# First mixer's attention: values held still, turned probabilities streamed, heads written turned, GpSimd divides

## The reference, cut to what matters

```
def window_attention(q, k, v, k_ctx, v_ctx, sink):      # 8 heads of 64, 2 key/value heads, blocks of 128 queries
    s_loc = einsum(q, k) * scale, -inf outside |qpos - kpos| <= 128
    s_ctx = einsum(q, k_ctx) * scale                    # 256 context keys
    p = softmax(concat[s_loc, s_ctx, sink])[..., :-1]
    return p_loc @ v + p_ctx @ v_ctx

def attn_gmlp_mixer(h, hc, w_in, w_out, ...):
    q, k, v, ua, va = split(h @ w_in);  q, k = axial_rope(q), axial_rope(k)
    kc, vc = split(hc @ w_in[:, Q_W:Q_W + 2 * KV_W])
    attn = window_attention(q, k, v, kc, vc, sink)
    mix = chunk_gmlp(ua, va, w_s, b_s)                  # gelu, normalise, mix 128 tokens per group, gate
    return concat([attn, mix]) @ w_out                  # added to x under a gate row, followed by the expert FFN
```

## Time and profile before

| | |
|---|---|
| time, median of three runs | 2689.07 us (2686.43 to 2693.46) |
| span of the profiled execution | 2685.7 us |
| TensorE busy over the span | 2368.8 us (88%) |
| VectorE, ScalarE, GpSimd busy | 1851.2, 1218.2, 640.2 us |
| the attention's transposes begin | 115.76 us |
| the first output block begins | 144.94 us |
| the next stage's first instructions | 175.98 us |

### The profile page before, as it was taken

The page is one execution under the profiler, slowest core; times in us unless marked ns, Lnnn a source line. Parts: engine busy times, 40 slices in busy tenths (PEclk is TensorE's granted clock), DMA queues, the critical chain, the costliest instruction groups (busy, mean ns, idle before and its releaser), DMA issues. The chain is left out here.

```text
span 2685.7 us, 35259 instructions
## 1 busy us (share of the span) xinstructions
PE 2368.8 (88%) x12931; PEld 1574.4 (59%) x12932; DVE 1851.2 (69%) x3447; ACT 1218.2 (45%) x2591; POOL 640.2 (24%) x547
## 2 busy tenths in 40 slices
PE   6988778888888988888778799999999998968999
PEld 4774333443334444343332278898888887856887
DVE  4768776678567776867765566675666666797665
ACT  3433434444445544444434454456445444445543
POOL 0003444453444444455544300000000000003000
PEclk9999999999999999999999999999999999988999
DMA  9799999999999999999999945542555554312553
GB/s 390 282 385 418 404 427 427 422 427 426 424 404 412 389 423 414 426 427 427 427 423 425 427 158 187 187 157 95 184 185 179 188 187 167 104 50 112 186 185 114
DMA packets 121706, 811.27 MB, mean 302 GB/s; under 512 B 15713, under 2 KB 18825, under 8 KB 26584
## 3 DMA queue, kind: packets, MB, share of 16 engines
q0 software_dynamic: 74160, 540.05, 48.2%
q1 hardware_dynamic: 47400, 269.32, 27.9%
HBM read 807.12 MB, written 1.15 MB: 301 GB/s over the span
## 5 line engine op out<-in xcount | busy, mean ns | idle before, releaser
L1451 PE MATMUL bank<-rows,diag 128*128 128x512 f32 (+1 forms) x2060 | 995.2, 620 | 216.3 <-ACT diag L1607 215.9
L1849 DVE CUSTOM_DVE_ANT_0 rows<-rows,h 128x1024 f32<-128x1024 f32 (+1 forms) x512 | 620.0, 1224 | 360.4 <-DMA rows<-in_peer_rows,idx 354.4
L1451 PEld LDWEIGHTS bank<-rows,diag 128*128 128x128 f32 (+1 forms) x2060 | 371.5, 194 | 743.0 <-ACT diag L1607 421.8
L1330 POOL DMA_INDIRECT rows<-in_peer_rows,idx x512 | 604.7, 1181 | 747.3 <-PE bank L1451 685.9
L1598 ACT ACTIVATE picks<-picks 128x1 f32<-128x1 f32 (+1 forms) x512 | 103.3, 202 | 638.9 <-DVE picks L1849 618.3
L2194 PE MATMUL bank<-hT_pair,halves 128*128 128x512 f32 x864 | 307.2, 398 | 0.4 <-DVE hT_pair L2072 0.4
L2195 PE MATMUL bank<-hT_pair,halves 128*128 128x256 f32 x864 | 242.2, 280 | 0.0
L1607 ACT ACTIVATE diag<-const_table,picks 128x128 f32<-128x128 f32 (+1 forms) x512 | 205.5, 401 | 48.0 <-ACT picks L1602 1.1
L2128 DVE TENSOR_TENSOR halves<-weight_ring,halves 128x2048 fp32r<-128x2048 f32 x73 | 167.0, 2288 | 72.3 <-ACT halves L2123 72.1
L2194 PEld LDWEIGHTS bank<-hT_pair,halves 128*128 128x128 f32 x864 | 162.3, 188 | 40.8 <-DVE hT_pair L2072 1.0
L1363 PE MATMUL bank<-halves_b,halves_a 128*128 128x256 f32 x912 | 171.5, 330 | 0.6 <-issue 0.6
(11 more groups left out here) (592 smaller groups left out, 3761.8 us busy)
## 6 DMA issues: line engine op xcount, KB each, us to landing
weight_ring<-in_ffn_w_gate SPq DMA_DIRECT2D x44, 1024.0 KB, 5.0
weight_ring<-in_ffn_w_up SPq DMA_DIRECT2D x44, 1024.0 KB, 4.8
weight_ring<-in_ffn_w_down SPq DMA_DIRECT2D x44, 1024.0 KB, 4.8
mod_ring<-in_mod_w SPq DMA_DIRECT2D x16, 1024.0 KB, 8.8
weight_ring<-in_peer_w_q SPq DMA_DIRECT2D x16, 1024.0 KB, 9.5
half_ring<-in_mod_w SPq DMA_DIRECT2D x24, 512.0 KB, 6.9
rows<-in_mod_w SPq DMA_DIRECT2D x12, 1024.0 KB, 9.1
weight_ring<-in_attn_w_in SPq DMA_DIRECT2D x12, 1024.0 KB, 4.8
```

The source lines that it names most:

```text
L1330: nc.gpsimd.indirect_dma_start(ring[:, s], None, dram["peer_rows"], bass.IndirectOffsetOnAxis(ap=idx[:, T, n:n + 1], axis=0)).then_inc(row ...
L1451: mm = nc.tensor.matmul(bank[:, :], diag[0:n, j % DIAG_SLOTS], ring[0:n, j % ROW_SLOTS, D + half * 512:D + (half + 1) * 512], start=(j in ...
L1849: dotted.up(nc.vector.tensor_tensor_reduce(out=ring[r, s, 0:D], in0=ring[r, s, 0:D], in1=its_h, scale=1.0, scalar=0.0, op0=ALU.mult, op1=A ...
```

## The change

The probabilities are divided before they are turned: `factor(T)` on VectorE makes the reciprocals, and GpSimd, idle in this stage until now, multiplies the 16 units in place; the transposes wait for it (`evened`). `mix` takes a pair of heads: the 64 value columns are held still, the turned probabilities (128 columns) are streamed, the two value halves go to partitions 0 to 63 and 64 to 127 of the same bank. The heads come out turned, in pairs, so the turns of the attention's halves, `scale` and its write to `cat` go; `high_cat` and `low_cat` read banks 4 and 5 directly, and the rows of `attn_out_w` are reordered on the host to match.

The orders change with it: the second eight exponentials stand ahead of the last emptying and the GELUs; the output product's first half (both token tiles) stands ahead of `mix_tokens`; one chunk stands ahead of the two remaining turns; the last three half loads stand behind the output blocks in SyncE's queue; four accumulations move into the loop of output blocks (two for each of the first two). The core of the diff:

```
+                def mix(pair):
+                    T, c = pair // GQA, pair % GQA
+                    wait_copied(2 * pair)
+                    wait_copied(2 * pair + 1)
+                    for s in range(4):
+                        for v in range(2):
+                            a = v * HD
+                            values = proj[:, s, Q_W + KV_W + a:Q_W + KV_W + a + HD] if s < NT else kvc[:, s - NT, KV_W + a:KV_W + a + HD]
+                            mm = nc.tensor.matmul(kit.bank[4 + T][a:a + HD, c * P:(c + 1) * P], values, PT[:, (2 * pair + v) % 4, s, :],
+                                                  start=(s == 0), stop=(s == 3), skip_group_check=True)
...
-                    pe.wait_ge(exped.sem, x0 + j + j // HEADS + 1)
+                    pe.wait_ge(evened.sem, ev0 + j + 1)
...
+                    if j in (4, 8, 12):
                         rows.multiply(pe, 1)
...
+                first_half = [(T, k) for T in range(NT) for k in range(4)]
+                product(nb, bank(0), ready=ready, steps=first_half, starts=((0, 0),))
                 mix_tokens()
-                turn_cat(1)
-                wait_copied(2 * HEADS - 1)
-                product(nb, bank(0), ready=ready, steps=every[:4])
+                rows.multiply(pe, 1)
                 turn_cat(2)
                 turn_cat(3)
-                rows.multiply(pe, 2)
-                product(nb, bank(0), ready=ready, steps=every[4:]).then_inc(W.multiplied, 1)
+                rows.multiply(pe, 1)
+                product(nb, bank(0), ready=ready, steps=[(T, k + 4) for T, k in first_half], starts=()).then_inc(W.multiplied, 1)
```

ScalarE:

```
                 exps(0)
                 empty(5)
+                exps(1)
                 empty(6)
                 act.wait_ge(emptied.sem, emptied_at(6))
                 for a in (v0, u0):
                     gelued.up(...)
-                exps(1)
                 for j in range(HEADS, 2 * HEADS):
                     ...
-                    if j == HEADS + 4:
+                    if j == HEADS + 3:
                         high_cat(0)
                     if j == HEADS + 5:
-                        kit.roots(act, [(stat[:, 3], stat[:, 2])])
-                    if j == HEADS + 6:
                         make_high(nb)
+                kit.roots(act, [(stat[:, 3], stat[:, 2])])
                 for j in range(1, 4):
                     high_cat(j)
```

VectorE and GpSimd:

```
+                factor(0)
                 rows.add(dve, 4)
...
                 for j in range(HEADS):
+                    if j == 2:
+                        factor(1)
                     ...
-                rows.accumulate(dve, 3)
-                scale(0)
                 normal = norm_values()
                 next(normal)
-                rows.accumulate(dve, 1)
                 low_cat(0)
+                make_low(nb)
+                rows.accumulate(dve, 2)
                 next(normal)
-                make_low(nb)
-                scale(1)
+                low_cat(1)
                 join(0)
                 join(1)
                 rows.add(dve, 4)
-                for j in range(1, 4):
-                    low_cat(j)
+                low_cat(2)
+                low_cat(3)
                 make_low(nb + 1)
                 for j in range(no):
                     if j < 2:
-                        rows.accumulate(dve, 1)
+                        rows.accumulate(dve, 2)
...
+            @block.gpsimd
+            def _(pool):
+                for T in range(NT):
+                    pool.wait_ge(factored.sem, f0 + T + 1)
+                    for u in range(T * HEADS, (T + 1) * HEADS):
+                        evened.up(nc.gpsimd.tensor_scalar(probs(u), probs(u), soft[:, 7, u:u + 1], None, ALU.mult))
```

SyncE:

```
                 rows.fetch(sp, 1)
-                rows.fetch_halves(sp, 3)
                 sp.wait_ge(mixed.sem, mi0 + HEADS)
                 W.issue(sp, b0 + nb + 2)
                 rows.fetch(sp, 2)
                 sp.wait_ge(mixed.sem, mi0 + len(units))
                 W.issue(sp, b0 + nb + no)
+                rows.fetch_halves(sp, 3)
                 kit.load(sp, vec[:, 2], rows.row(0, 3))
```

More of the change, by code:

```diff
@@ L704, in last_product, with product @@
                     mm.then_inc(W.multiplied, 1)
-                def product(b, out, between={}, ready=at_once, steps=every):
+                def product(b, out, between={}, ready=at_once, steps=every, starts=((0, 0), (1, 0))):
                     pe.wait_ge(split.sem, p0 + b + 1)
@@ L712, in product @@
                             mm = nc.tensor.matmul(out[:, T, :], t[:, k, T * P:(T + 1) * P], w[:, k, :],
-                                                  start=(k == 0 and n == 0), stop=(k == KD - 1 and n == 2), skip_group_check=True)
+                                                  start=((T, k) in starts and n == 0), stop=(k == KD - 1 and n == 2), skip_group_check=True)
                         if (T, k) in between:
@@ L778, in turn_probs @@
                     probs_turned.up(mm)
-                def mix(j):
-                    T, h = units[j]
-                    wait_copied(j)
-                    a = h // GQA * HD
-                    for c in range(4):
-                        values = proj[:, c, Q_W + KV_W + a:Q_W + KV_W + a + HD] if c < NT else kvc[:, c - NT, KV_W + a:KV_W + a + HD]
-                        mm = nc.tensor.matmul(kit.bank[4 + T][:, h * HD:(h + 1) * HD], PT[:, j % 4, c, :], values,
-                                              start=(c == 0), stop=(c == 3))
-                    mixed.up(mm)
+                def mix(pair):
[8 more added lines that the diff above has]
+                                                  start=(s == 0), stop=(s == 3), skip_group_check=True)
+                            if s == 3:
+                                mixed.up(mm)
                 def turn_cat(j):
                     T, k = TURNS[j]
-                    pe.wait_ge(written.sem, w0 + {0: 1, 1: 2, 2: 4, 3: 4}[j])
+                    pe.wait_ge(written.sem, w0 + 2)
                     for i in range(4):
@@ L824, in _ @@
                 turn_probs(1)
-                for j in range(len(units)):
+                for j in range(0, len(units), 2):
                     if j + 2 < len(units):
                         turn_probs(j + 2)
-                    mix(j)
-                    if j in (3, 9, 12):
+                        turn_probs(j + 3)
+                    mix(j // 2)
+                    if j in (4, 8, 12):
                         rows.multiply(pe, 1)
-                    if j == HEADS + 3:
-                        turn_cat(0)
                 def ready(T, k):
@@ L880, in high_cat @@
                     T, k = TURNS[j]
-                    act.wait_ge(turned.sem, t0 + 6 + j)
+                    if j < 2:
+                        act.wait_ge(mixed.sem, mi0 + HEADS * (j + 1))
+                    else:
+                        act.wait_ge(turned.sem, t0 + 4 + j)
                     cat_high.up(nc.scalar.copy(x_hi[:, k:k + 4, T * P:(T + 1) * P],
@@ L4034 @@
         elif name in BLOCKED:
+            if name == "attn_out_w":
+                heads = a[..., :Q_W, :].reshape(2, GQA, HD, D).swapaxes(0, 1).reshape(a.shape[:-2] + (Q_W, D))
+                a = _np.concatenate([heads, a[..., Q_W:, :]], -2)
             a = a.reshape(a.shape[:-2] + (KD, P, a.shape[-1] // BLK, BLK))
```

20 lines of the change are left out of this document (8 added, 12 removed).

## The result

The changed kernel takes 2701.29 us (median of 5 runs, 2698.68 to 2705.58) against 2691.0 us for the kernel before (5 runs, 2686.43 to 2693.46): ratio 1.0047, 95% interval 1.0034 to 1.0060. It is 10 us slower, and 1.3 us above the range. The profiled execution has a span of 2700.8 us (before 2685.7) and a time of 2702.99 us.

The account below looks back on a forecast made before the run. It took TensorE and the DMA engines (share 0.98) as nearly full in this stage. +1.0 us (TensorE and VectorE) and +1.5 (DMA) made 2689.07 + 2.5 = 2691.5 us, chance 0.42; range 2683 to 2700.

Parts of the forecast that it names:

- The half loads' place: SyncE's queue: loads behind output blocks wait for accumulation 21, delaying chunks 15 and 16; cost 1.0 to 2.0, taken 1.5 us.
- nothing carries over: Stage end: w_q's last load would end near 181, before the next stage's chunks are requested (178.9 + 2.5).
- The division: GpSimd, attention: 0.9 us per unit, second eight done at 126.4, hidden from TensorE.
- rival 3: GpSimd becomes the bound at turn 15 from 1.4 us a division; 2695.5 us at 1.8, 2703.5 at 2.36; chance 0.13.
- The last value product: TensorE, attention: ends at 137.5 instead of 142.6, 5.1 us won.
- wait for x_low: First output block: TensorE waits 3.2 us for low_cat(1), queued on VectorE behind accumulations and normalisation.
- The first value product: TensorE, attention: moves from 118.25 to 119.9, behind the emptying of bank 0 and turn 3.
- row addition: After token mixing: the chunk ahead of the two turns waits for rows.add, ending 147.6, and runs 147.7 to 148.7.
- block 1 and block 2 late on VectorE: Output blocks: block 1 0.6 us late; VectorE needs 6.2 us per 5.76 us block, so the stage is 1.0 us late.
- Rival 4: Value products: halves don't lie side by side, a pair costs 1.94 us; +3.4 beyond the forecast, 2695 us; chance 0.10.
- Rival 1: The win survives: the low_cat(1) wait and late chunk vanish, about 4.6 of 5.1 us stay, 2684.5 us; chance 0.15.
- Rival 2: DMA is no bound: SyncE's stall costs nothing; +1.0 us or a little under, 2689.5 us; chance 0.20.

Follow-up runs that it names:

- run 10: Kernel before with only the three half loads put behind the output blocks and their accumulations moved as in the change; 2699.52 us, ratio to before 1.0042.
- run 6: Changed kernel with queue orders mended on several engines, GpSimd still dividing all sixteen units; 2690.51 us, ratio to before 1.0001.
- run 11: Changed kernel with orders mended and the division split, ten units on GpSimd and six on VectorE; 2688.51 us, ratio to before 1.0001.
- Run 9: Changed kernel with the last three half loads and their accumulations put back where they stood; 2692.21 us, ratio to before 1.0016.
- run 12: Kernel before, unchanged, profiled once more for the scatter between executions; 2690.01 us (one measurement).
- run 7: Changed kernel with the loops of mix turned, so the value halves no longer alternate; 2703.13 us, ratio to before 1.0050.

## Why the prediction was wrong

It had the mechanisms and mis-sized two of them, both on the side of slower.

*The half loads' place* is the term that failed: "cost it 1.0 to 2.0 us", and "nothing carries over". Alone it measured 7.7 us at the gather (run 10): 4.1 at the end of the stage, and 3.5 carried over. The forecast saw the gap (nothing in the DMA queues from 148 to 156) and then charged only what TensorE would see at the next two chunks. TensorE waited 3.05 us there instead of 1.5, but its wait is not the price of the gap (in run 10 it waits 2.0). The DMA engines were at 0.98 before, behind them the next stage needs its first rows, and 3.5 MB not moved in the gap are moved later: the late loads are issued 4.6 us after the next stage's start instead of 2.95, and from that start to the gather it takes 33.1 us instead of 30.9. The argument that w_q's last load ends in time looked at one load, not at the bytes. I had read the row that tells it, a share of 0.98 in both windows, and did not carry it into this sum.

*The division*: taken at 0.9 us, it takes 1.56 to 2.42, in the mean 1.62 with its gaps. That is above the point of 1.4 us which rival 3 named: the sixteen take 25.87 us, and TensorE waits (0.38, 1.00, 0.84). Two sums of rival 3 don't follow from its own numbers: at 1.8 us a division, 110.9 + 28.8 is 139.7, 6.2 us late and not 5; and 4.6 us late, if 3 fall into waits as at its upper end, give 2693 and not 2695. The last value product ends 3.0 us behind the forecast. The Trainium skill's figure (GPSIMD Engine Reference, section 3.1: 769 ns) is half of what was measured. With the other orders mended it costs about 2 us of stage and nothing measurable in the time (runs 6 and 11).

*Between those two*, 1.6 us more are lost by the product's end. Around the wait for x_low the granted clock fell (0.92 in this window): the four steps behind it take 2.43 us instead of 1.44 and the first eight instructions of token mixing 1.55 instead of 0.95. Run 9 had shorter waits and kept 1.00; but run 12 fell to 0.92 behind a wait of 1.15 us. I had no term for it.

*What held.* The first value product (4.45 against 4.1 from the transposes) behind the emptying of bank 0; 16 instructions in 1.03 us against 1.15; the wait for x_low, 2.94 against 3.2, and for the row addition, 1.78; block 1 and block 2 late on VectorE; SyncE blocked at the third half load. Rival 4 is out (1.03 us a pair; run 7 shows the halves side by side). Rival 1 did not happen: TensorE can be 5.2 us earlier at the last value product (run 11), but no order tried carried more than 1.4 us of it to the gather. Rival 2, "DMA is no bound", was given 0.20 and is the contrary of what the runs show. Rival 3 was right in its place and in its sign, and too small.

An exclusive lock between GpSimd and VectorE's two-input work, which rival 3 weighed with the Trainium skill's SBUF — State Buffer, section SBUF: two separate sides, would stop one side for the whole of the other's instruction. The trace shows less than that, and nothing regular: two products of the normalisation take 1.74 us beside a division and 1.29 otherwise, one accumulation 1.71 instead of 1.28 beside a division that keeps its 1.56, and the longest division takes 2.42 beside an accumulation that keeps its 1.28. In run 11 an accumulation (126.62, 1.27 us) and a division (126.05, 1.57 us) overlap for 1.0 us and neither is longer than alone. What decides which side stretches stays open.

```profile
130.32 1.74 DVE L994 TENSOR_TENSOR proj<-proj,stat 128x512 f32<-128x512 f32 x2
132.10 1.60 DVE L996 TENSOR_TENSOR h<-proj 128x1024 f32<-128x1024 f32 x1
```

## What to carry to other kernels

Where the DMA engines are near full, price a blocked queue by the bytes it doesn't move until the next point that needs them all (here right to about 2 us of 8), not by the wait of the engine next in line; and follow it past the end of the stage. A load into a ring waits for the consumer that frees its buffer, so moving either in its queue moves both, and everything queued behind. A faster step on one engine need not reach the end of a stage whose transfers are near full: here 5.2 us of TensorE time became 0.1 to 0.5 at the gather. That the transfers alone take the rest isn't shown, since waits for VectorE (2.0 us) and a blocked queue early in the stage (some 2 us of bytes) had their part.

## What the hardware showed that was not expected

GpSimd's multiplication by a value for each partition costs 0.60 us for 128 columns and 1.56 for 512, about 2.5 ns a column, more than the 1.33 that a two-input product of the earlier trace rows gives when scaled. VectorE does the same 512 columns in 0.47 to 0.91 us (run 11, the longer ones beside a division on GpSimd). Two column halves of TensorE overlap even when they don't alternate, over about four instructions at the seam (run 7): 1.51 us a pair, between 1.03 alternating and the 1.94 of no overlap at all. And the clock's fall in this stage came in one of two profiles of the same kernel, so the 1.6 us that it cost the changed kernel can't be tied to a wait.
